# Splitting weights ahead of two norms, taking two chunks part by part, and a new start, in a kernel of two transformer blocks

## What is computed

```python
h = x + hybrid_mixer(rmsnorm(x, g), w_in, pool_w, ..., w_out)
h = h + conv_ffn(rmsnorm(h, g), w_up, conv_w, conv_b, w_down)
x = rmsnorm(h, norm_final_g)
for i in range(2):
    sx1, cx1, gx1, sx2, cx2, gx2 = split(silu(c) @ ada_w[i] + ada_b[i])
    hx = rms(x, norm_mix_g[i]) * (1 + cx1) + sx1
    x = x + gx1 * mixer_i(hx, ...)
    x = x + gx2 * (relu(modulate(rms(x, norm_mlp_g[i]), sx2, cx2) @ w1[i]) ** 2 @ w2[i])
```

## Time and profile before

| | us |
|---|---|
| median of three runs | 1358.7 (1356.49 to 1359.45) |
| the profiled execution, its own time | 1358.1 |
| its span in the profile | 1356.2 |
| TensorE busy | 1315.9 (97%) |
| VectorE busy | 825.6 (61%) |
| ScalarE busy | 594.2 (44%) |
| GpSimd busy | 423.1 (31%) |

### The profile page before, as it was taken

One profiled execution on the slowest core, in us unless ns is written; L12 is line 12 of the kernel. 1 busy time (PEld: TensorE's weight loads), 2 busy tenths in 40 slices (PEclk: granted clock), 3 DMA queues, 4 the chain that ended last, 5 costly groups with the idle time before them and its releaser, 6 DMA issues.

```text
span 1356.2 us, 19950 instructions
## 1 busy us (share of the span) xinstructions
PE 1315.9 (97%) x7832; PEld 1107.6 (82%) x7832; DVE 825.6 (61%) x1263; ACT 594.2 (44%) x952; POOL 423.1 (31%) x435
## 2 busy tenths in 40 slices
PE   5999999999999999989999999999899999999999
PEld 5888898899886788858878888787577777999887
DVE  6678577899876545286533444343667765755553
ACT  4335545566654233243321243222545554666432
POOL 2443221222411001244400044111466552388200
PEclk9999999999999999999999999999999999999999
DMA  6778347865555222244433443334523220545552
GB/s 256 247 256 286 125 176 278 300 210 184 181 178 204 78 94 78 94 175 166 156 140 140 144 151 141 140 140 165 189 82 109 94 93 32 194 181 185 186 186 78
DMA packets 63963, 220.06 MB, mean 162 GB/s; under 512 B 6912, under 2 KB 10240, under 8 KB 63872
## 3 DMA queue, kind: packets, MB, share of 16 engines
q1 hardware_dynamic: 63584, 218.56, 45.2%
q10 hardware_dynamic: 288, 0.25, 0.1%
HBM read 217.73 MB, written 1.05 MB: 161 GB/s over the span
## 4 chain that ended last, share of the span: by engine, by line
PE 89%; DVE 6%; issue 2%; ACT 1%; POOL 1%; DMA 1%; ACTq 0%; DVEq 0%; POOLq 0%
PE ps L523 23%; PE ps L537 22%; PE ps L535 22%; PE ps L513 7%; PE ps L515 4%; PE ps L578 2%; PE ps L900 1%; DVE wlo L1481 1%; PE ps L927 1%; PE ps L914 1%; DVE A L1925 1%; DVE tmp L1940 1%; PE ps L893 1%; POOL ssum_c L2136 1%; DVE tmp L1748 1%
## 5 line engine op out<-in xcount | busy, mean ns | idle before, releaser
L523 PE MATMUL ps<-A,whi 128*128 128x256 f32 (+2 forms) x1612 | 532.3, 330 | 9.5 <-ACT A L1043 6.7
L537 PE MATMUL ps<-A,wlo 128*128 128x256 f32 (+2 forms) x1568 | 501.2, 320 | 0.6 <-DVE wlo L1481 0.6
L535 PE MATMUL ps<-A,whi 128*128 128x256 f32 (+2 forms) x1568 | 501.1, 320 | 0.0
L1481 DVE TENSOR_TENSOR wlo<-raw,whi 128x1024 fp32r<-128x1024 f32 x305 | 387.9, 1276 | 99.9 <-ACT whi L1018 99.8
L1018 ACT ACTIVATE whi<-raw 128x1024 fp32r<-128x1024 f32 x305 | 319.8, 1050 | 281.2 <-PE ps L537 159.1
L523 PEld LDWEIGHTS ps<-A,whi 128*128 128x128 f32 x1612 | 306.4, 190 | 71.3 <-issue 29.3
L535 PEld LDWEIGHTS ps<-A,whi 128*128 128x128 f32 x1568 | 298.4, 190 | 22.5 <-issue 1.7
L537 PEld LDWEIGHTS ps<-A,wlo 128*128 128x128 f32 x1568 | 298.3, 190 | 22.4 <-DVE wlo L1481 1.2
L513 PE MATMUL ps<-H,whi 128*128 128x512 f32 x432 | 152.0, 397 | 0.0
L2125 POOL TENSOR_TENSOR H<-tmp,H 128x256 fp32r<-128x256 f32 (+1 forms) x86 | 121.0, 1407 | 61.1 <-ACT H L1313 40.7
L515 PE MATMUL ps<-H,wlo 128*128 128x256 f32 x432 | 120.8, 280 | 0.0
(11 more groups left out here) (274 smaller groups left out, 1412.7 us busy)
## 6 DMA issues: line engine op xcount, KB each, us to landing
raw<-in_ada SPq DMA_DIRECT2D x96, 512.0 KB, 4.3
raw<-in_w SPq DMA_DIRECT2D x64, 512.0 KB, 3.4
raw<-in_w_up SPq DMA_DIRECT2D x44, 512.0 KB, 4.3
raw<-in_w_in SPq DMA_DIRECT2D x38, 512.0 KB, 5.2
raw<-in_w_0a SPq DMA_DIRECT2D x32, 512.0 KB, 3.6
raw<-in_w_0b SPq DMA_DIRECT2D x32, 512.0 KB, 3.5
raw<-in_na_in SPq DMA_DIRECT2D x24, 512.0 KB, 6.1
raw<-in_w_down SPq DMA_DIRECT2D x22, 512.0 KB, 3.5
```

Source lines behind the costliest of these rows:

```text
L523: e.matmul(o, w_hi, ah, start=k == 0, stop=False)
L535: e.matmul(o, w_hi, al, start=False, stop=False)
L537: m = e.matmul(o, w_lo, ah, start=False, stop=last)
L1481: e.tensor_tensor(wlo[i % NRAW][:, :cols], raw[i % NRAW][:, :cols], plain(whi[s % NHI][:, :cols]), SUB).then_inc(S("wlo").sem, 1)
```

## The change

- *Plan.* Of the modulation units ahead of w1_0a and na_in, three are loaded ahead of the stage's first two units and the rest behind them; the order of use (`TAKEN`) is kept. Weights 0 and 1 of both stages get their high and low splits during the last units of the stage before (high parts with units 5 and 6, low parts with units 6 and 7 of ab_out; high parts with units 13 and 14, low parts with units 14 and 15 of w2_0b). The third weight's high split comes behind the norm's high parts.
- *Norm steps.* `norm_whole` makes all sixteen halves in one row into eight tiles `xn` that lie in the hidden tile's space; then DVE makes the low parts of chunks 3 to 7, and POOL those of chunks 0 to 2.
- *First two chunks.* `first_two` takes chunks 0 and 1 of w1_0a and na_in together: for each part k both chunks' high and low weights by the high activation (four products), and at the end the low activations, chunk 0 and then chunk 1.
- *Order at the norms.* In both, the sum of the partial squares now stands ahead of the first two modulation units, and the sum of the last square behind them.
- *Start.* TensorE takes ten products of zeros (`warm_up`); `par` is issued ahead of the ones; the squares of the second half of x go from POOL to ACT, behind the high split of unit 1, and their sums to DVE, behind the low split of unit 1; in the first chunk the low weights come in one row behind the high products.
- *Layout.* High and low parts of one chunk lie next to each other in `A`, `H` and `Z`; the joint products read one piece of 512 columns.
- na_in's biases are loaded at another place of the queue.

```diff
@@ -46,6 +46,10 @@
 ADA_STEPS = 96
 ADA_BEFORE = {"ab_in": 6, "w1_0a": 6, "na_in": 8}
+AHEAD = {"w1_0a": 3, "na_in": 3}
+LOW_P = range(3)
 ADA_AFTER = {"w_in": (6, 22), "w_out": (0, 48), "w_up": (2, 42)}
...
+            here = following[name, u] = []
             if u > first and (u - first) % 2 and n < upto:
-                plan += [("ada", n), ("ada", n + 1)]
-                n += 2
-            if name in MOD_AFTER and (u % 2 == 0 or name == "w1_0a" and u in (5, 11)):
-                assert n in MOD
-                plan.append(("ada", n))
-                n += 1
-    assert n == ADA_STEPS
-    return plan
-PLAN = weight_plan()
+                modulation(2, here)
+            owed += name in MOD_AFTER and (u % 2 == 0 or name == "w1_0a" and u in (5, 11))
+            if ahead and u == 1:
+                modulation(ADA_BEFORE[name] - ahead, front[name])
+            if not ahead or u:
+                assert not owed or n in MOD
+                modulation(owed, here)
+                owed = 0
+        order += front[name]
+        for u, i in enumerate(at):
+            order += [i, *following[name, u]]
+    assert n == ADA_STEPS and sorted(order) == list(range(len(plan)))
+    return plan, front, following, order
+PLAN, FRONT, FOLLOWING, TAKEN = weight_plan()
+TAKEN_AT = {i: e for e, i in enumerate(TAKEN)}
 UNIT = {key: i for i, key in enumerate(PLAN)}
...
-    for i, (name, _) in enumerate(PLAN):
-        later = [s for s, at in enumerate(SPLIT) if at >= i][:3 if name == "ada" else 4]
-        upto = min(later[-1] + 1 if later else len(SPLIT), sum(at < i + NRAW for at in SPLIT))
+    issued, last = [], -1
+    for i in range(len(PLAN)):
+        last = max(last, TAKEN_AT[i - NRAW]) if i >= NRAW else last
+        issued.append(last)
+    for e, i in enumerate(TAKEN):
+        later = [s for s, at in enumerate(SPLIT) if TAKEN_AT[at] >= e][:3 if PLAN[i][0] == "ada" else 4]
+        upto = min(later[-1] + 1 if later else len(SPLIT), sum(issued[at] < e for at in SPLIT))
         hi[i] = range(n_hi, max(n_hi, upto))
         n_hi = max(n_hi, upto)
-        ahead = max(n_hi - 1, sum(at <= i for at in SPLIT))
+        behind = 0 if e + 1 < len(TAKEN) and any(TAKEN[e + 1] == FRONT[x][0] for x in AHEAD) else 1
+        ahead = max(n_hi - behind, sum(TAKEN_AT[at] <= e for at in SPLIT))
         lo[i] = range(n_lo, max(n_lo, ahead))
         n_lo = max(n_lo, ahead)
...
@@ -282,12 +306,17 @@
     whi = [sb(f"whi{i}", 1024, f32r) for i in range(NHI)]
     R = sb("R", 8 * 512).rearrange("p (c t) -> p c t", c=8)
-    A = sb("A", 2 * 8 * 512, f32r).rearrange("p (x c t) -> p x c t", x=2, c=8)
-    Ahi, Alo, A2 = A[:, 0], A[:, 1], A.rearrange("p x c t -> p c x t")[:, :, :, 0:256]
+    A = sb("A", 2 * 8 * 512, f32r)
+    Ahi, Alo = [A.rearrange("p (c x t) -> p x c t", x=2, t=512)[:, x] for x in range(2)]
+    Bhi, Blo = [A[:, 0:4096].rearrange("p (c x t) -> p x c t", x=2, t=256)[:, x] for x in range(2)]
+    E_hi, E_lo = [A[:, 4096:8192].rearrange("p (c x t) -> p x c t", x=2, t=256)[:, x] for x in range(2)]
+    B2 = A[:, 0:4096].rearrange("p (c y) -> p c y", y=512)
+    Ehi, Elo = [A[:, 8 * 258 * i:8 * 258 * (i + 1)].rearrange("p (c t) -> p c t", c=8) for i in range(2)]
     h_at = here[0]
     here[0] += 65536
     H = sb("H", 2 * 8192, f32r, at=h_at)
-    Hhi, Hlo, H2 = H[:, 0:8192], H[:, 8192:16384], H.rearrange("p (x c t) -> p c x t", x=2, t=256)
+    H2 = H.rearrange("p (c y) -> p c y", y=512)
     par = sb("par", N_PARAMS)
     con = sb("con", N_CONSTS)
...
     z2 = h32("z2", 2048, 38912).rearrange("p (c t) -> p c t", c=8)
...
@@ -463,11 +491,11 @@
             if i == 44:
                 e.dma_start(seqs, dram["seqs"]).then_inc(S("seqs").sem, 16)
             load(i)
-            at = i - (NRAW - 1)
-            if at == UNIT["na_in", 0] - 1:
+            if PLAN[i] == ("na_in", 5):
                 for h in range(4):
                     load_bias(h)
+            at = i - (NRAW - 1)
             if at > 0 and PLAN[at][0] == "na_in":
                 _, scores, _ = attend2(PLAN[at][1])
...
@@ -544,6 +572,29 @@
                     if end and following:
                         following(blk // 8)
+        def first_two(name, T, acts, hi_ready, lo_ready):
+            tiles = []
+            for n in range(2):
+                g, s = CHUNK_AT[name, n], SPLIT_AT[name, n]
+                signal, count = bank_left(*CHUNKS[g - 3])
+                w.wait_ge(S(signal), count)
+                tiles.append((s, T[n], ps[g % 3][:, :T[n]]))
+            for k in range(8):
+                hi_ready(k)
+                c = slice(128 * k, 128 * k + 128)
+                for s, Tn, o in tiles:
+                    w.wait_ge(S("whi"), s + 1)
+                    e.matmul(o, whi[s % NHI][:, c], acts(k)[0][:, :Tn], start=k == 0, stop=False)
+                    low_ready(s)
+                    e.matmul(o, wlo[SPLIT[s] % NRAW][:, c], acts(k)[0][:, :Tn], start=False, stop=False)
+            for s, Tn, o in tiles:
+                for k in range(8):
+                    lo_ready(k)
+                    m = e.matmul(o, whi[s % NHI][:, 128 * k:128 * k + 128], acts(k)[1][:, :Tn], start=False, stop=k == 7)
+                m.then_inc(S("mm").sem, 1)
         def low_ready(s):
             w.wait_ge(S("wlo"), s + 1)
...
@@ -644,6 +693,13 @@
             m.then_inc(S(st + "_row").sem, 1)
+        def warm_up():
+            zeros = cond.rearrange("p k m -> p (k m)")
+            w.wait_ge(S("cond0"), 1)
+            for _ in range(10):
+                e.matmul(ps[7][:, :256], zeros[:, :128], zeros, start=True, stop=True)
         def first_chunk():
...
@@ -667,9 +723,8 @@
             high(range(4))
             low(range(4))
-            weight_low(range(4))
             high(range(4, 8))
-            weight_low(range(4, 8))
+            weight_low(range(8))
             low(range(4, 8)).then_inc(S("mm").sem, 1)
...
@@ -855,14 +911,15 @@
         linear("ab_out", 512, lambda k: (Ahi[:, k], Alo[:, k]), C_hi, C_lo)
         w.wait_ge(S("D_x"), 4)
+        column_sums("m0", ssum, 0, "_part", 6)
         ada_before("w1_0a", 0, 2)
-        column_sums("m0", ssum, 0, "_part", 6)
         column_sums("m0", sq[1], 4, "_sq", 8).then_inc(S("m0_sum").sem, 1)
         ada_before("w1_0a", 2, 4)
         column_rows("m0")
         ada_before("w1_0a", 4)
+        first_two("w1_0a", (512, 512), lambda k: (Ahi[:, k], Alo[:, k]), ready("m0_hi", 2), ready_low("m0_lo", "m0_lp", 2))
         linear("w1_0a", 512, lambda k: (Ahi[:, k], Alo[:, k]), ready("m0_hi", 2), ready_low("m0_lo", "m0_lp", 2),
-               during=lambda n: mod_summed("w1_0a", n))
+               during=lambda n: mod_summed("w1_0a", n), begin=2)
         linear("w2_0a", 512, lambda k: Hc(k, 512), ready("h0a_hi"), ready("h0a_lo"), during=lambda n: written("w2_0a", n))
         linear("w1_0b", 512, lambda k: (Ahi[:, k], Alo[:, k]), ready("m0_hi", 2), ready_low("m0_lo", "m0_lp", 2),
...
         w.wait_ge(S("m0_t"), 16)
+        column_sums("na", ssum, 0, "_part", 6)
         ada_before("na_in", 0, 2)
-        column_sums("na", ssum, 0, "_part", 6)
+        column_sums("na", sq[1], 4, "_sq", 8).then_inc(S("na_sum").sem, 1)
         ada_before("na_in", 2, 4)
-        column_sums("na", sq[1], 4, "_sq", 8).then_inc(S("na_sum").sem, 1)
         ada_before("na_in", 4, 6)
         column_rows("na")
...
@@ -953,8 +1010,10 @@
             if scores:
                 scores2(*scores)
+        first_two("na_in", (512, 256), lambda k: (Ahi[:, k], Alo[:, k]), ready("na_hi", 2), ready_low("na_lo", "na_lp", 2))
+        during_na(1)
         linear("na_in", lambda n: 256 if NA_CHUNKS[n][0] == "q" else 512, lambda k: (Ahi[:, k], Alo[:, k]), ready("na_hi", 2),
-               ready_low("na_lo", "na_lp", 2), during=during_na, midway=lambda n: after_na(n - 1))
+               ready_low("na_lo", "na_lp", 2), during=during_na, midway=lambda n: after_na(n - 1), begin=2)
         def out_part(n, pairs):
...
-            e.activation(Ahi[:, 4 + g, LEFT], pooled[:, g], ACT.Copy).then_inc(S("B_hi").sem, 1)
+            e.activation(Bhi[:, 4 + g], pooled[:, g], ACT.Copy).then_inc(S("B_hi").sem, 1)
         for what, i in walk("w_in"):
             if what == "unit":
-                his(UNIT["w_in", i])
+                for s in HI_AT[UNIT["w_in", i]]:
+                    hi(s)
+                    if s == 1:
+                        e.activation(squares[1].rearrange("p (c t) -> p c t", c=4), R[:, 4:8, LEFT],
+                                     ACT.Square).then_inc(S("squares_act").sem, 1)
                 if i - 1 in VALUES:
                     out1_hi(VALUES[i - 1])
...
@@ -1295,13 +1359,8 @@
                     square_whole("m0", "about_r", 7)
         w.wait_ge(S("m0_v"), 1)
         e.activation(column[:, 4:8], column[:, 0:4], ACT.Sqrt).then_inc(S("m0_r").sem, 1)
-        his(before("w1_0a")[0])
         for c in range(8):
-            if c == 1:
-                his(before("w1_0a")[1])
-            if c == 4:
```

(59 more changed lines are left out.)

81 lines of the change are left out of this document (40 added, 41 removed).

## The result

The change makes the kernel faster, but by much less than forecast: median 1354.54 us (1352.3 to 1358.31) against 1358.7, ratio 0.9974 with a 95% interval of 0.9962 to 0.9987, from seven executions of each kernel. In a later set on one chip it was 0.997 (0.9958 to 0.9982). The forecast was 1344.1.

What follows compares the result with a forecast made beforehand. TensorE was busy 97% of the span, leaving 40 us idle or at lower clock to win. Gains of 5.4 (start), 5.6 (m0) and 3.6 (na) made 14.6 us: 1344.1 against 1358.7, range 1340.5 to 1349.5.

Steps and rivals of the forecast that it cites:

- Start: First chunks of w_in: POOL squares moved, zeros' products, sooner `par`; chunk 3 starts near 21.7, gain 5.4 us.
- full clock: Upper bound at the start: TensorE at full clock from 9.9 on, gain 5.4 us; the case taken.
- half clock as before: Lower bound at the start: TensorE at half clock past 19, chunk 3 starts at 24.5, gain 2.6 us.
- Rival 1: Start stays slow: clock back at half after the zeros' products; 2.8 us less gain, 1346.9, chance 0.17.
- Norms: Values in one row, then low halves, at m0 and na: gains of 5.6 us and 3.6 us.
- the sum: Gains of start, m0 and na added: 5.4 + 5.6 + 3.6 = 14.6 us, giving 1344.1 us.
- rival 2: DVE and POOL collide in both norms: ten low halves at up to 1.0 us, 1353.1; at 0.8, 1349; chance 0.13.
- rival 3: Given back later: 1 to 3 us lost in attention behind na and by half clock elsewhere; 1346, chance 0.1.
- The clock at m0: Modulation units between one-column products keep full clock at m0; row 0.9 us sooner, gain 5.6 instead of 4.7.
- Layout: Joint products reading 512 columns in one piece: no gain or loss; pair already at 0.347 us.
- The late load of na_in 4: Unit 4's load at na waits for chunk 0's end: costed at nothing, at worst 0.2 us.
- Rival 4: Slower than before: joint products read 512 columns slower as one piece, from 30 ns each; 1360, chance 0.04.

Runs made afterwards that it cites:

- two_no_zeros: pool_two without the ten products of zeros at the start: median 1338.81 us, ratio 0.9867 against the kernel before.
- gaps: The changed kernel with a wait and a small VectorE copy from PSUM between VectorE's low halves: median 1343.13 us, ratio 0.9895 against the kernel before.
- start_alone: The kernel before with only the new start of the changed kernel: median 1350.54 us, ratio 0.9953 against the kernel before.
- two_old_sums: pool_two with the column sums of both norms in their old order: median 1340.74 us, ratio 0.9884 against the kernel before.
- after_again: The changed kernel run again unaltered, in a later set on one chip: median 1352.80 us, ratio 0.9970 against the kernel before.
- pool_two: The changed kernel with POOL making the low parts of chunks 0 and 1 only, VectorE the rest: median 1337.94 us, ratio 0.9853 against the kernel before.
- vector_waits: The changed kernel with VectorE's ten low halves waiting until POOL's six are done: median 1341.75 us, ratio 0.9881 against the kernel before.
- two_pool_squares: pool_two with the squares of x's second half and the additions back on POOL: median 1342.65 us, ratio 0.9903 against the kernel before.

## Why the prediction was wrong

*Start: right in mechanism, 5.4 forecast, 6.7 measured.* The squares off POOL are the large term, as costed. I had split the rest badly: between "full clock" and "half clock as before" I put 2.8 us; two_no_zeros shows 1.2, since the clock rises sooner anyway. And I took 0.45 us for the sooner load of `par`: ScalarE starts at 5.92 instead of 7.64, 1.7 sooner, and what it waits for now is x. That accounts for most of the 1.3 us above the forecast (the first product starts at 8.80, where the forecast had 9.9). Rival 1 did not come: from 8.8 on the products run at full clock. ScalarE's timeline in the changed kernel, answering to the earlier trace rows:

```profile
5.92 1.71 ACT L1088 ACTIVATE A<-R,par 128x256 fp32r<-128x256 f32 x4 [2.96 <-DMA R<-in_x]
```

*Norms: wrong, and this is the step that failed.* The prediction put "POOL's six low halves (8.3 us in before, from 585.33 to 593.69) begin with chunk 0 and are done by 591". The row arrived as forecast (values from 575.09, forecast 575.1 once the 6.5 us gained so far are taken off), and the values took 6.4 us, not 6.6. VectorE's ten low halves took 4.04, not 5.5. But POOL's fifth subtraction took 6.89 where I carried over the 0.73 to 0.90 of before, so POOL was done at 590.86 where the sum, moved by the same gains, had 583.6. Chunk 2 of w1_0a started at 597.04, where the sum had 589.3: 7.7 late. The head sum in na started at 964.62, where the sum had 958.9: 5.7 late. Together 13.4 us, against 1.3 won at the start; what remains up to the end is in the traces too. The changed kernel is 2.5 us ahead at the head sum and 3.6 at the end. It gives back 1.6 behind na, 0.5 on the head sum at half clock and 1.1 by a new fall of the clock near 996; it gets 1.5 because the kernel before is at half clock near 1154 and this one isn't, and about 1.6 from the layout (below).

I had the right rule and the right rows and drew the wrong side from them. I read the spread of L1925 as "VectorE gets slower beside POOL" and priced rival 2 as ten slow halves. The other side, that VectorE's row can hold up POOL, has no term in the sum and no rival. In before no subtraction took over 0.90 us: of the ten low halves two pairs stood between values that read PSUM, but the last six stood in a row, and POOL got in there as well. So the missing breaks explain the loss only in part: gaps shows that breaks would have let POOL in, and the row of six shows that a row need not keep it out. The step of the change that made the long row was in my own working: "The normed values go in one row", "then ten low halves on DVE".

*The range* was added up wrong. By its own terms, rival 1 (2.8), rival 3 (1.9) and rival 2 at 0.8 (4.9), its upper end is 1353.7, not 1349.5. That the measured 1354.54 lies near this is luck: rival 2 priced VectorE's low halves, which in fact were faster than the sum had them.

*The clock at m0*: I took the full clock there, with the separated sums as the reason. It held up to the pause. Whether the order is the reason is open, though the traces lean that way: the eight entries that make the row took 1.16 us, at full clock, in all nine traces with the new order, and of the three with the old order 2.08 in before, 1.80 in start_alone and 1.16 in two_old_sums. TensorE's timeline in start_alone:

```profile
572.04 1.80 PE L643 MATMUL ps<-ssum,con 128*128 128x128 f32 x8 [0.23 <-DVE ssum L1938]
```

*Layout: right in w_down, wrong in w2_1.* Ten pairs in w_down still take 3.47 us. Timeline of the changed kernel, answering to the earlier trace rows:

```profile
380.12 0.39 PE L541 MATMUL ps<-H,whi 128*128 128x512 f32 x1
...
383.59 0.39 PE L541 MATMUL ps<-H,whi 128*128 128x512 f32 x1
```

But w_down's pair is not that of w2_1, a later stage with joint products. Timelines of TensorE in w2_1, ten pairs each, first of the kernel before, then of the changed one:

```profile
1299.67 0.40 PE L513 MATMUL ps<-H,whi 128*128 128x512 f32 x1
...
1303.20 0.40 PE L513 MATMUL ps<-H,whi 128*128 128x512 f32 x1
```

```profile
1296.71 0.39 PE L541 MATMUL ps<-H,whi 128*128 128x512 f32 x1
...
1300.17 0.39 PE L541 MATMUL ps<-H,whi 128*128 128x512 f32 x1
```

A pair takes 0.353 us there before and 0.347 after. It is 0.353 in both traces with the old layout (before, start_alone) and 0.347 in the ten with the new one. For the 256 pairs of w2_1 this is about 1.6 us (in the traces), a term that the sum put at nothing; no run changes the layout alone.

*The late load of na_in 4: right that it costs nothing.* ScalarE stood idle for it, but TensorE didn't wait for chunk 1's square. ScalarE's timeline in the changed kernel:

```profile
966.58 1.06 ACT L1077 ACTIVATE whi<-raw 128x1024 fp32r<-128x1024 f32 x1 [2.34 <-DMA raw<-in_na_in]
```

Rival 3 shows in this one profile (the 1.6 us given back behind na) and not in that of after_again, which is 4.3 us ahead of the kernel before at the head sum and 4.3 once the attention is over. Rival 4 did not show. pool_two, the change with one number and the counts that follow from it altered, is 19 to 20 us faster than before, 1.4% or more, and beats both kernels; that is 4 to 6 us more than the sum of 14.6, so the sum was not only wrong about POOL: its other terms were too small.

## What to carry to other kernels

When two engines get in each other's way, don't only ask how much slower each instruction gets; ask where the other has a break. Interleaving that looks untidy (values and low parts in turns) may be what lets the second engine in, and tidying it into one row can starve that engine for the row's whole length, whatever little work it has left. Don't count on the opposite either: the row of six in the kernel before let POOL in. Give the second engine less work, so that it finishes ahead of the row (pool_two), or let the row wait for it (vector_waits).

## What the runs showed of the hardware

- A POOL subtraction of 128x256 with two inputs takes 0.74 us beside VectorE instructions that read one tensor from PSUM, and 6.89 and 6.86 us beside an unbroken row of twelve with two SBUF inputs; it ends 0.59 us after that row in both cases. A PSUM copy of 0.21 us behind each low half, with a wait ahead of it, brings it to 1.07. Inside a row of six of the kernel before it took 0.90.
- It goes both ways: POOL's instructions of 1024 columns stretch four VectorE instructions from 1.67 to 6.43 us (two_pool_squares).
- The Trainium skill, "GPSIMD Engine Reference", Specifications, names the contention and its condition (two SBUF inputs). These rows agree: 0.74 us beside values that read PSUM, 6.89 beside low halves that read SBUF twice.
- After a pause of 6.15 us TensorE ran at half clock for over 6 us of unbroken products, which adds about 3 us to the pause (6.13 for fourteen products that take 3.2 at 0.23 each). After a pause of 6.16 us in after_again it added about 1.7.
- A pair of a joint product (512 columns) and a low weight's (256) takes 0.353 us in w2_1 where its high and low activations lie apart, and 0.347 where they are neighbours; in w_down it takes 0.347 either way.
